# Weight sums of the FFN's fast products: which engine forms them, and in which order

## The chip, the cores and the metric

The kernel runs on 1 core of one Trainium2 chip. The time is device time of one execution in microseconds (us), and the time of a version is the median of its runs. Engines: PE is TensorE, DVE VectorE, ACT ScalarE, POOL GpSimd, SP SyncE, whose queue issues the loads. PEld is PE's weight load.

## The reference

Two layers over a sequence of 256 tokens with 2048 channels, each a mixer and a SwiGLU FFN with norms around them. The change touches the FFN alone:

```python
def swiglu(h, w_gate, w_up, w_down):          # 2048 -> 5632 -> 2048
    return (jax.nn.silu(h @ w_gate) * (h @ w_up)) @ w_down

h = rms_norm(x, norm_ffn_pre[layer])
f = swiglu(h, ffn_w_gate[layer], ffn_w_up[layer], ffn_w_down[layer])
x = x + rms_norm(f.astype(x.dtype), norm_ffn_post[layer])
```

## The kernel before

**Precision.** Every 512x512 weight tile is loaded as f32 (1 MiB, `raw`), copied by ACT to `w_hi` (L1051, `hi`), and DVE takes the rest as `w_lo` (L1791, `lo`). The left operand is split too, and a product is three passes, hi x hi, w_lo x hi, w_hi x lo, of 4 matmuls with 512 columns for each half of the tokens. There are 4 `w_hi` and 3 `w_lo` buffers, so `hi` of a unit waits for the unit four before it and `lo` for the one three before it.

**The FFN.** Its 5632 hidden channels are 11 blocks of 512. The first goes through the ordinary path (the head), the other 10 are bodies. A body computes gate and up of its block (2048 x 512 each) for 2 token tiles by seven-product (Strassen-like) 2x2 forms in place of eight: products P1 to P7, each over two pairs of weight tiles, A (rows 0 and 1) and B (rows 2 and 3). A quarter product (L1635, printed by the tiles sc, pv or acc of L1490) is 12 matmuls. Then the gated tile of the block before is transposed (`turn`, L1701, matmuls of L1504), and multiplied with four tiles of w_down, d0 to d3 (`down`, L1676, L1696), 24 matmuls each. A body has 14 quarter products, 4 downs and 8 transposes. The order of the 18 units is written out in `ENTRIES` (L100) and in the lists of each engine.

**Weight sums.** Of the weight tiles g0 to g3 and u0 to u3 the products need running sums, formed in the raw buffer itself: P5 = g(first) + u(first), P6 adds u(second), P4 adds g(second); P7 = u(first) + u(second). So there are 8 sums a body. `form` (L1794, L1804) does one on DVE; `transfer` (L2333, L2347) does one by an accumulating DMA from SBUF to SBUF that POOL issues. Before: four by `FORMS` (P5A, P6A, P6B, P4B) and four by `TRANSFERS` (P5B, P7A, P7B, P4A).

**Buffers.** 8 raw buffers serve the 12 loads of a body. `place_loads` (L586) gives each load, in the order of `LOADS`, the buffer whose tile is released first by the plan; SP waits for that release and issues in order.

**First bodies.** A layer's first body has lists of its own (`first_block`), since the left operands' combinations S1 to S4 for both pairs are formed there: `left_total`, `left_high` on ACT (L1267) and `left_low` on DVE (L1855, L1857), which all later bodies reuse. ACT's `copy` (L1291) moves a bank's partial result aside, `unload` (L1317) drains a down's bank to `yacc`, `seed` (L1309) writes it back as the start of the next body's down. `head_end` (L343) is the order of the two units ahead of the first body.

Of the kernel before, what the change touches and what calls it, by code (L numbers as in the profile page):

```python
# [51 lines left out]
RAW, HI, LO = 3, 4, 3  # L52
# [34 lines left out]
class Slot:  # L87


    def __init__(self, u, kg, n, first, last, w, cb=0, region="h", layer=0):  # L90
# [69 lines left out]
def loads_of(body):  # L160

    return FIRST_LOADS[len(EARLY):] if body.first else LOADS

# [179 lines left out]
def head_end(slots, body):  # L343
# [16 lines left out]
    tasks += half(gate, 1) + gate.post + half(up, 0) + [Task("early_load", src=body, what=name) for name in EARLY[2:]] + [total(TOTALS[3]), Task("spill", 2 * body.layer + 1, slot=up)]  # L360
    tasks += high_ahead(gate.u, up) + half(up, 1) + low_ahead(gate.u, up) + up.post
# [224 lines left out]
def place_loads(plan):  # L586
# [25 lines left out]
    for part in plan.parts:  # L612
        for task in part.tasks or ():
            if task.kind == "early_load":
                take((task.src.index, task.what), range(RAW) if task.what in EARLY[2:] else (RAW + EARLY.index(task.what),), released(task.src, task.what))
            elif task.kind == "tile_unit" or task.kind == "half" and task.t == 0 and task.passes[0] == 0:
                take(task.slot.u, (POST_GAIN,) if task.slot.u in plan.last_ups else range(RAW), (("lo", task.slot.u + 1, task.slot.u),))
# [12 lines left out]
def trunk(nc, x, norm_mix_pre, norm_mix_post, norm_ffn_pre, norm_ffn_post,  # L630
# [9 lines left out]
    with ExitStack() as ctx:  # L640
# [378 lines left out]
        def _(act):  # L1019
# [299 lines left out]
            def block(body):  # L1319
# [8 lines left out]
                unload(body.prev, 2, 0)  # L1328
                seed(body, 0, 1)
                unload(body.prev, 2, 1)  # L1330
                high(body, "P5A")
                seed(body, 1, 0)
                block_high(body, 0)
                block_high(body, 1)
                high(body, "d1")
                copy(body, "P1")
                high(body, "P5B")
                unload(body, 0, 0)
                seed(body, 1, 1)
                unload(body, 0, 1)  # L1340
                high(body, "P6A")
                seed(body, 3, 0)
                high(body, "P6B")
                unload(body, 1, 0)
                seed(body, 3, 1)
                unload(body, 1, 1)
                high(body, "P3B")
                high(body, "P7A")
                copy(body, "P5")
                seed(body, 2, 0)  # L1350
# [4 lines left out]
                high(body, "d3")  # L1355
# [4 lines left out]
                unload(body, 3, 0)  # L1360
                seed(body, 2, 1)
                unload(body, 3, 1)
                high(body, "d2")
                if body.next:
                    seed(body.next, 0, 0)
                high_next("P1B")
                high_next("P1A")
                silu_part(body, 0)
                silu_part(body, 1)
                high_next("d0")  # L1370

            def first_block(body):

                block_high(body, 0)
                block_high(body, 1)
                high(body, "P5A")
                left_high("S1B", body.layer)
                high(body, "d1")
                unload(body, 0, 0)
                high(body, "P5B")  # L1380
                unload(body, 0, 1)
                copy(body, "P1")
                left_high("S2A", body.layer)
                left_high("S4A", body.layer)
                high(body, "d3")
                high(body, "P6A")
                unload(body, 1, 0)
                high(body, "P6B")
                unload(body, 1, 1)
                copy(body, "P5")  # L1390
                left_high("S2B", body.layer)
                left_high("S4B", body.layer)
                high(body, "P3B")
                high(body, "P7A")
                left_high("S3A", body.layer)
                left_high("S3B", body.layer)
                high(body, "P7B")
                copy(body, "P6")
                high(body, "P3A")
                high(body, "P2A")  # L1400
                high(body, "P4A")
                copy(body, "P7")
                high(body, "P2B")
                unload(body, 3, 0)
                unload(body, 3, 1)
                high(body, "P4B")
                high(body, "d2")
                seed(body.next, 0, 0)
                high(body.next, "P1B")
                high(body.next, "P1A")  # L1410
                silu_part(body, 0)
                silu_part(body, 1)
                high(body.next, "d0")
# [984 lines left out]
```

## Time and profile before

| | us |
|---|---|
| median of 3 runs | 2158.71 (2158.47 to 2160.74) |
| the profiled execution | 2158.62 |
| its span in the profile | 2156.8 |
| PE busy | 2141.2 |
| DVE busy | 1698.2 |
| ACT busy | 1489.6 |
| POOL busy | 230.7 |

The FFN bodies run from 422 to 1030 us and from 1516 to 2124 us. A timeline row gives the start, the duration from the first start to the last end of the merged instructions, engine, line, operation, what is written from what, the count, and in brackets idle time ahead with what ended it. Matmuls overlap, so the distance of two starts says more of PE than a duration.

### The profile page before, as it was taken

How to read it: one execution, taken by the hardware profiler on the slowest of the kernel's cores; microseconds unless marked ns; L12 is line 12 of the kernel's file. 1: busy time of each engine (PE TensorE's matmuls, PEld its weight loads, DVE VectorE, ACT ScalarE, POOL GpSimd, SP SyncE). 2: the span in 40 equal slices, each digit the busy share in tenths (PEclk: the TensorE clock that was granted, in tenths of full speed). 3: DMA queues.
4: the chain of work that ended last, by engine and by line, in shares of the span. 5: the costliest groups of instructions: out<-in, count | busy, mean ns of one | idle time of the engine just before them, and what ended most of it. 6: DMA issues, size and time to landing. Idle time of an engine off the chain costs nothing.

```text
span 2156.8 us, 26554 instructions
## 1 busy us (share of the span) xinstructions
PE 2141.2 (99%) x9771; PEld 1765.4 (82%) x9771; DVE 1698.2 (79%) x1538; ACT 1489.6 (69%) x1774; POOL 230.7 (11%) x274
## 2 busy tenths in 40 slices
PE   9999999999999999999999999999999999999998
PEld 7888888888888888888887787788888888888886
DVE  5577466898898888888755656678998888888886
ACT  6677544787777777777655555447777777777774
POOL 0851000000000000000021001001000000000001
PEclk9999999999999999999999999999999999999999
DMA  9545445799989999997564454557999999998993
GB/s 315 189 154 194 145 148 198 255 290 298 266 256 263 282 296 276 285 289 230 183 215 146 149 169 143 177 175 239 278 299 273 275 292 279 281 292 266 263 263 149
DMA packets 226559, 508.82 MB, mean 236 GB/s; under 512 B 13736, under 2 KB 16384, under 8 KB 214656
## 3 DMA queue, kind: packets, MB, share of 16 engines
q1 hardware_dynamic: 214192, 422.68, 55.6%
q0 software_dynamic: 11520, 83.89, 19.7%
q8 instruction: 79, 1.29, 0.2%
q10 hardware_dynamic: 720, 0.56, 0.1%
q14 instruction: 48, 0.39, 0.0%
HBM read 416.92 MB, written 6.29 MB: 196 GB/s over the span
## 4 chain that ended last, share of the span: by engine, by line
PE 95%; DVE 2%; issue 1%; ACT 1%; DMA 1%; SPq 0%; ACTq 0%; POOLq 0%; POOL 0%; DVEq 0%
PE acc L1477 34%; PE acc L1696 20%; PE sc L1490 20%; PE pv L1490 10%; PE acc L1490 5%; PE tp L1504 3%; PE sc L1590 1%; DVE w_lo L1791 1%; PE pv L1619 1%; PE sc L1586 1%; PE pv L1614 1%; DMA raw<-in_ev_w_in 0%; PE sc L1569 0%; PE pv L1569 0%; ACT h_hi L1097 0%
## 5 line engine op out<-in xcount | busy, mean ns | idle before, releaser
L1791 DVE TENSOR_TENSOR w_lo<-raw,w_hi 128x2048 fp32r<-128x2048 f32 x263 | 601.6, 2293 | 100.2 <-PE acc L1477 41.5
L1051 ACT ACTIVATE w_hi<-raw 128x2048 fp32r<-128x2048 f32 x263 | 503.7, 1916 | 120.4 <-PE acc L1477 45.6
L1477 PE MATMUL acc<-w_hi,h_hi 128*128 128x512 f32 x936 | 261.4, 401 | 2.6 <-ACT h_hi L1021 2.6
L1477 PE MATMUL acc<-w_lo,h_hi 128*128 128x512 f32 x936 | 252.2, 391 | 0.2
L1477 PE MATMUL acc<-w_hi,h_lo 128*128 128x512 f32 x936 | 251.1, 390 | 0.0
L1791 DVE TENSOR_TENSOR w_lo<-xs,w_hi 128x2048 fp32r<-128x2048 f32 x88 | 201.2, 2288 | 31.3 <-PE acc L1696 20.4
L1477 PEld LDWEIGHTS acc<-w_lo,h_hi 128*128 128x128 f32 x936 | 175.6, 188 | 38.9 <-DVE w_lo L1791 1.4
L1477 PEld LDWEIGHTS acc<-w_hi,h_lo 128*128 128x128 f32 x936 | 175.5, 188 | 37.0
L1477 PEld LDWEIGHTS acc<-w_hi,h_hi 128*128 128x128 f32 x936 | 171.1, 189 | 37.0 <-issue 5.5
L1051 ACT ACTIVATE w_hi<-xs 128x2048 fp32r<-128x2048 f32 x88 | 168.5, 1915 | 23.9 <-PE acc L1490 8.1
L1317 ACT ACTIVATE yacc<-acc 128x512 f32<-128x512 f32 x160 | 95.0, 595 | 113.3 <-PE acc L1696 113.3
L1696 PE MATMUL acc<-w_hi,y_lo 128*128 128x512 f32 x640 | 171.0, 389 | 0.0
L1696 PE MATMUL acc<-w_hi,y_hi 128*128 128x512 f32 x640 | 171.0, 389 | 0.0
L1696 PE MATMUL acc<-w_lo,y_hi 128*128 128x512 f32 x640 | 171.0, 389 | 0.0
L1791 DVE TENSOR_TENSOR w_lo<-gq,w_hi 128x2048 fp32r<-128x2048 f32 x54 | 123.5, 2288 | 24.4 <-PE acc L1696 19.6
L1696 PEld LDWEIGHTS acc<-w_hi,y_hi 128*128 128x128 f32 x640 | 120.1, 188 | 24.9
L1696 PEld LDWEIGHTS acc<-w_lo,y_hi 128*128 128x128 f32 x640 | 120.1, 188 | 24.9
L1696 PEld LDWEIGHTS acc<-w_hi,y_lo 128*128 128x128 f32 x640 | 120.1, 188 | 24.9
L1791 DVE TENSOR_TENSOR w_lo<-queries,w_hi 128x2048 fp32r<-128x2048 f32 x50 | 114.4, 2287 | 15.5 <-PE acc L1696 10.2
L1051 ACT ACTIVATE w_hi<-gq 128x2048 fp32r<-128x2048 f32 x54 | 103.5, 1917 | 23.6 <-DVE gq L1804 11.6
L1791 DVE TENSOR_TENSOR w_lo<-gx,w_hi 128x2048 fp32r<-128x2048 f32 x46 | 105.2, 2288 | 15.6 <-PE acc L1696 10.2
L1490 PE MATMUL sc<-w_hi,h_hi 128*128 128x512 f32 x400 | 108.9, 394 | 0.0
(299 smaller groups left out, 3615.6 us busy)
## 6 DMA issues: line engine op xcount, KB each, us to landing
raw<-in_od_w_in SPq DMA_DIRECT2D x48, 1024.0 KB, 5.1
raw<-in_ffn_w_gate SPq DMA_DIRECT2D x38, 1024.0 KB, 9.7
raw<-in_ev_w_in SPq DMA_DIRECT2D x37, 1024.0 KB, 5.3
raw<-in_ffn_w_up SPq DMA_DIRECT2D x36, 1024.0 KB, 7.8
raw<-in_ffn_w_down SPq DMA_DIRECT2D x36, 1024.0 KB, 6.6
xs<-in_ffn_w_up SPq DMA_DIRECT2D x22, 1024.0 KB, 8.0
xs<-in_ffn_w_down SPq DMA_DIRECT2D x18, 1024.0 KB, 7.2
xs<-in_ffn_w_gate SPq DMA_DIRECT2D x18, 1024.0 KB, 10.2
```

Of the source, the lines that this page charges most:

```text
L1051: act.activation(w_hi[u % HI][:, :, :], raw[place.buf][:, :, :], ACT.Copy).then_inc(hi_done, 1)
L1317: act.activation(yacc[:, t, j * KC:(j + 1) * KC], down_banks[k], ACT.Copy).then_inc(drained[k], 1)
L1477: mm = pe.matmul(acc[n % 2][t][:, :], operand(lhs, a, k, t), w[:, k, :], start=first and k == 0 and j == 0, stop=last and k == KT - 1 and ...
L1490: mm = pe.matmul(bank, a[:, k, :], w[:, k, :], start=start and k == 0 and j == 0, stop=stop and k == KT - 1 and j == 2, skip_group_check=c ...
L1504: ins = pe.transpose(dst, src, ident[:, :])
L1586: mm = pe.matmul(sc[:, t, :], q[:, kt, t * P:(t + 1) * P], k[:, kt, task.i % 2, :], start=True, stop=True)
L1590: mm = pe.matmul(sc[:, :, :].rearrange("p m t -> p (m t)"), q[:, kt, t * P:(t + 1) * P], k[:, kt, :, :].rearrange("p m t -> p (m t)"), sta ...
L1614: mm = pe.matmul(pv[:, 0, t * HD:(t + 1) * HD], probT[:, j, t * P:(t + 1) * P], v[:, j, task.i * HD:(task.i + 1) * HD], start=j == 0, stop ...
L1619: mm = pe.matmul(pv[:, 0, 0:CV], flat_pt[:, j * P:(j + 1) * P], v[:, j, hd * CV:(hd + 1) * CV], start=j == 0, stop=j == 1)
L1696: mm = pe.matmul(down_banks[k], a[:, kt, t * P:(t + 1) * P], w[:, kt, :], start=body.first and i == 0 and kt == 0, stop=i == 2 and kt == K ...
L1791: dve.tensor_tensor(w_lo[u % LO][:, :, :], raw[plan.place[u].buf][:, :, :], w_hi[u % HI][:, :, :].bitcast(F32), ALU.subtract).then_inc(lo_ ...
```

## The change

Three sums of a body go by accumulating DMA (P7B, P7A, P4B), five on DVE (P5A, P5B, P6A, P6B, P4A). P5A's sum is formed one body ahead, for a first body in the head. The units get another order: P1A first, the transposes split (four behind P1A, four behind P1B), downs in the order d1, d0, d2, d3, three of them early and d3 at the end. Loads, seeds, unloads, copies and the first half of the gating follow that order. The first body and the others no longer have different load lists.

```diff
-ENTRIES = ("P1B", "P1A", "d0", "P5A", "d1", "P5B", "P6A", "P6B", "P3B",
-           "P7A", "P7B", "P3A", "P2A", "d3", "P4A", "P2B", "P4B", "d2")
-FIRST_ENTRIES = ("P1B", "P1A", "d0", "P5A", "d1", "P5B", "d3", "P6A", "P6B", "P3B",
-                 "P7A", "P7B", "P3A", "P2A", "P4A", "P2B", "P4B", "d2")
-DOWNS = ("d0", "d1", "d3", "d2")
-LOADS = ("d0", "g2", "u2", "g0", "u1", "u0", "d1", "u3", "g1", "g3", "d3", "d2")
-FIRST_LOADS = ("d0", "g2", "u2", "g0", "u0", "d1", "u1", "u3", "d3", "g1", "g3", "d2")
-EARLY = FIRST_LOADS[:4]
-FORMS = ("P5A", "P6A", "P6B", "P4B")
-TRANSFERS = ("P5B", "P7A", "P7B", "P4A")
+ENTRIES = ("P1A", "P1B", "d1", "P5A", "P5B", "d0", "P6A", "d2", "P6B",
+           "P3B", "P3A", "P7A", "P7B", "P2A", "P4A", "P2B", "P4B", "d3")
+FIRST_ENTRIES = ("P1A", "P1B", "d1", "P5A", "d0", "P5B", "d2", "P6A", "P6B",
+                 "P3B", "P3A", "P7A", "P7B", "P2A", "P4A", "P2B", "P4B", "d3")
+DOWNS = ("d1", "d0", "d2", "d3")
+LOADS = ("g2", "g0", "u0", "d1", "u2", "d2", "u3", "d0", "u1", "g3", "g1", "d3")
+EARLY = LOADS[:3]
+FORMS = ("P5A", "P5B", "P6A", "P6B", "P4A")
+FORMS_AHEAD = FORMS[:1]
+TRANSFERS = ("P7B", "P7A", "P4B")
...
-    tasks += high_ahead(gate.u, up) + half(up, 1) + low_ahead(gate.u, up) + up.post
+    tasks += high_ahead(gate.u, up) + half(up, 1)
+    tasks += [Task("form", src=body, what=name) for name in FORMS_AHEAD] + up.post + low_ahead(gate.u, up)
```

The new lists that the prediction walks through: DVE's of a middle body, and the ends of the first body's on DVE and ACT.

```python
# DVE, block
gated(body.prev, 1)
low(body, "d1")
form(body, "P5B")
block_low(body, 0)
low(body, "P5A")
block_low(body, 1)
low(body, "P5B")
form(body, "P6A")
low(body, "d0")
form(body, "P6B")
low(body, "P6A")
low(body, "d2")
low(body, "P6B")
low(body, "P3B")
form(body, "P4A")
low(body, "P3A")
low(body, "P7A")
low(body, "P7B")
low(body, "P2A")
upper_part(body, 0)
low(body, "P4A")
low(body, "P2B")
upper_part(body, 1)
low(body, "P4B")
low(body, "d3")
low_next("P1A")
if body.next:
    form(body.next, "P5A")
gated(body, 0)
low_next("P1B")
```

```python
# DVE, first_block, from P3B on      # ACT, first_block, from P3B on
low(body, "P3B")                     # high(body, "P3B")
low(body, "P3A")                     # high(body, "P3A")
left_low("S3A", body.layer)          # copy(body, "P6")
low(body, "P7A")                     # left_high("S3A", body.layer)
left_low("S3B", body.layer)          # left_high("S3B", body.layer)
low(body, "P7B")                     # high(body, "P7A")
form(body, "P4A")                    # high(body, "P7B")
low(body, "P2A")                     # high(body, "P2A")
```

## Rows read from the trace of the kernel before

**Rows 1.** The page: header, busy time of engines, chain by engine.
```profile
span 2156.8 us, 26554 instructions
...
PE 2141.2 (99%) x9771; PEld 1765.4 (82%) x9771; DVE 1698.2 (79%) x1538; ACT 1489.6 (69%) x1774; POOL 230.7 (11%) x274
...
PE 95%; DVE 2%; issue 1%; ACT 1%; DMA 1%; SPq 0%; ACTq 0%; POOLq 0%; POOL 0%; DVEq 0%
```

**Rows 2.** Timeline of PE, a middle body's turn, and the next one's.
```profile
911.48 1.03 PE L1504 MATMUL tp<-ident,tok 128*128 128x128 f32 x8
912.27 1.17 PE L1490 MATMUL sc<-w_hi,h_hi 128*128 128x512 f32 x4
913.27 1.07 PE L1490 MATMUL sc<-w_lo,h_hi 128*128 128x512 f32 x4
914.18 1.07 PE L1490 MATMUL sc<-w_hi,h_lo 128*128 128x512 f32 x4
...
972.21 1.03 PE L1504 MATMUL tp<-ident,tok 128*128 128x128 f32 x8
```

**Rows 3.** Windows: stretch, then busy us of each engine, clock, DMA share, GB/s.
```profile
422.50:486.40 63.90, 63.80 (x286) 52.53 (x285) 62.04 (x42) 46.33 (x43) 3.46 (x4) 1.00 0.93 290
911.70:972.40 60.70, 60.70 (x274) 50.34 (x273) 53.16 (x28) 47.01 (x43) 3.48 (x4) 1.00 0.92 277
```

The engines of a windows row are PE, PEld, DVE, ACT and POOL in this order; the first row is a first body, the second a middle one.

**Rows 4.** Timeline of PE, product P4A of the first body, layer 0.
```profile
469.60 1.07 PE L1490 MATMUL sc<-w_hi,h_hi 128*128 128x512 f32 x4
470.77 1.20 PE L1490 MATMUL sc<-w_lo,h_hi 128*128 128x512 f32 x4
...
473.65 1.07 PE L1490 MATMUL acc<-w_lo,h_hi 128*128 128x512 f32 x4
```

**Rows 5.** Timeline of DVE in that first body.
```profile
423.33 2.28 DVE L1791 TENSOR_TENSOR w_lo<-gx,w_hi 128x2048 fp32r<-128x2048 f32 x1
...
431.33 2.29 DVE L1791 TENSOR_TENSOR w_lo<-raw,w_hi 128x2048 fp32r<-128x2048 f32 x1 [0.78 <-ACT w_hi L1051]
...
443.07 2.29 DVE L1804 TENSOR_TENSOR queries<-queries,xs 128x2048 f32<-128x2048 f32 x1
...
456.22 0.69 DVE L1857 TENSOR_TENSOR lefts<-prob,lefts 128x512 fp32r<-128x512 f32 x1
456.82 2.28 DVE L1791 TENSOR_TENSOR w_lo<-raw,w_hi 128x2048 fp32r<-128x2048 f32 x1
...
464.03 2.28 DVE L1791 TENSOR_TENSOR w_lo<-gq,w_hi 128x2048 fp32r<-128x2048 f32 x1
466.23 2.28 DVE L1804 TENSOR_TENSOR queries<-queries,gx 128x2048 f32<-128x2048 f32 x1
468.44 2.28 DVE L1791 TENSOR_TENSOR w_lo<-raw,w_hi 128x2048 fp32r<-128x2048 f32 x1
```

**Rows 6.** Timeline of PE, transposes in runs of four at the layer boundary.
```profile
1078.57 0.38 PE L1504 MATMUL tp<-ident,xs 128*128 128x128 f32 x2
...
1078.92 1.18 PE L1477 MATMUL acc<-w_hi,h_hi 128*128 128x512 f32 x4
1079.94 1.08 PE L1477 MATMUL acc<-w_lo,h_hi 128*128 128x512 f32 x4
```

**Rows 7.** The page: DMA queues, packets, MB, share of 16 engines' span.
```profile
q1 hardware_dynamic: 214192, 422.68, 55.6%
q0 software_dynamic: 11520, 83.89, 19.7%
```

**Rows 8.** Timeline of ACT in the first body.
```profile
457.73 0.57 ACT L1291 ACTIVATE probT<-sc 128x512 f32<-128x512 f32 x1
458.20 1.91 ACT L1051 ACTIVATE w_hi<-xs 128x2048 fp32r<-128x2048 f32 x1
```

**Rows 9.** Line L904, all weight loads: from issue to landing.
```profile
DMA to landing us min/median/max: 4.9/7.2/17.3
```

**Rows 10.** Timeline of PE, behind the last transposes of layer 0's FFN.
```profile
1031.65 1.17 PE L1477 MATMUL acc<-w_hi,y_hi 128*128 128x512 f32 x4 [0.39 <-ACT y_hi L1260]
```

More of the change, by code:

```diff
@@ L160, in loads_of @@
 def loads_of(body):
-    return FIRST_LOADS[len(EARLY):] if body.first else LOADS
+    return tuple(name for name in LOADS if not (body.first and name in EARLY))
 class Part:
@@ L1326, in high_next @@
                         hi(u)
-                unload(body.prev, 2, 0)
-                seed(body, 0, 1)
[L1330 to L1337, printed above, removed]
+                unload(body.prev, 3, 0)
+                seed(body, 1, 1)
+                unload(body.prev, 3, 1)
@@ new lines, in block @@
+                high(body, "P5A")
+                seed(body, 0, 0)
+                block_high(body, 0)
+                high(body, "P5B")
+                block_high(body, 1)
+                high(body, "d0")
+                unload(body, 1, 0)
+                copy(body, "P1")
+                seed(body, 0, 1)
+                unload(body, 1, 1)
+                seed(body, 2, 0)
+                high(body, "P6A")
+                high(body, "d2")
+                copy(body, "P5")
+                high(body, "P6B")
@@ L1348, in block @@
                 high(body, "P7A")
-                copy(body, "P5")
-                seed(body, 2, 0)
                 high(body, "P7B")
                 copy(body, "P6")
-                high(body, "P3A")
+                high(body, "P2A")
+                high(body, "P4A")
+                if body.next:
+                    seed(body.next, 1, 0)
+                high(body, "P2B")
+                copy(body, "P7")
+                high(body, "P4B")
+                high(body, "d3")
+                high_next("P1A")
@@ L1359, in block @@
                 high(body, "P4B")
[L1360 to L1367, printed above, removed]
+                unload(body, 2, 0)
+                unload(body, 2, 1)
+                high(body, "d3")
+                seed(body.next, 1, 0)
+                high(body.next, "P1A")
+                high(body.next, "P1B")
                 silu_part(body, 0)
                 silu_part(body, 1)
[L1370 to L1413, printed above, removed]
+                high(body.next, "d1")
             act.dma_start(pre[:, :, :], pre_T).then_inc(pre_in, 16)
@@ L1426, in _ @@
                     block(body)
-                unload(part.bodies[-1], 2, 0)
-                unload(part.bodies[-1], 2, 1)
+                unload(part.bodies[-1], 3, 0)
+                unload(part.bodies[-1], 3, 1)
                 for t in range(NT):
@@ L1751, in first_block @@
                     quarter_product(body, "P4B")
-                    down(body, 2)
+                    down(body, 3)
+                def first_block(body):
+                    quarter_product(body, "P1A")
+                    turn(body, 0)
+                    quarter_product(body, "P1B")
+                    turn(body, 1)
+                    down(body, 1)
+                    quarter_product(body, "P5A")
+                    down(body, 0)
+                    quarter_product(body, "P5B")
+                    down(body, 2)
+                    quarter_product(body, "P6A")
+                    quarter_product(body, "P6B")
+                    quarter_product(body, "P3B")
+                    quarter_product(body, "P3A")
+                    quarter_product(body, "P7A")
+                    quarter_product(body, "P7B")
+                    quarter_product(body, "P2A")
+                    quarter_product(body, "P4A")
+                    quarter_product(body, "P2B")
+                    quarter_product(body, "P4B")
+                    down(body, 3)
                 first_block(part.bodies[0])
@@ L2199, in first_block @@
                 low(body, "P3B")
+                low(body, "P3A")
                 left_low("S3A", body.layer)
@@ L2352, in _ @@
                 for body in section.bodies or ():
-                    transfer(body, "P5B")
+                    transfer(body, "P7B")
                     transfer(body, "P7A")
-                    transfer(body, "P7B")
-                    transfer(body, "P4A")
+                    transfer(body, "P4B")
 def log_counts():
```

134 lines of the change are left out of this document (69 added, 65 removed).

## The prediction

> **What bounds the kernel now.** I read the page's header first: TensorE (PE) is busy 2141.2 us of the 2156.8 us span, and the chain that ended last is 95% PE [rows 1]; the granted clock of the bodies is 1.00, the 2.4 GHz level [rows 3]. Busy time can hide waiting inside long matmuls, so the next view is PE's timeline of one late FFN body: groups of four 512-column matmuls start every 0.907 us (226.7 ns each) with no idle in brackets, across products and downs alike [rows 2]. One body is 66 such groups and 8 transposes, 66 x 0.907 + 0.88 = 60.7 us, and the two turns of neighbouring bodies lie exactly that far apart (911.48 and 972.21) [rows 2]. So 18 of the 20 bodies hold no PE stall that a better feed could take away. The windows view of such a body says who is nearest to becoming the bound: VectorE (DVE) 53.16 us of 60.70, the DMA engines 92%, ScalarE (ACT) 47.01 [rows 3]. The first body of a layer is tighter: DVE 62.04 of 63.90 [rows 3]. There PE does stall once: the w_hi group starts at 469.60, the w_lo group at 470.77 instead of 470.51, and the fourth group behind 469.60 is at 473.65 instead of 473.23: 0.42 us late in all, restart included [rows 4]. The w_lo it waits for ended at 470.72, right behind a weight sum (466.23) in front of it [rows 5]. This is seen once per layer. So in the part that the diff touches, before can give back 2 x 0.42 = 0.8 us, and no more.
>
> **The change, part by part.** (1) *Matmuls.* The number is unchanged: 14 quarter products of 12 and 4 downs of 24 in each body. Only the order differs. No gain, no loss.
>
> (2) *The turn of the gated tile.* Before, its 8 transposes are one run; after, 4 stand behind P1A and 4 behind P1B. The run of 8 takes from 911.48 to 912.27, and the group after the next starts 1.00 us on instead of 0.907: 0.79 + 0.10 = 0.89 us [rows 2]. Runs of four stand at the layer boundary: 1078.57 to 1078.92, then 1.02 us, so 0.35 + 0.11 = 0.46, and 0.47 with the last hundredth of the restart [rows 6]. Two of them cost 0.94, so a body is 0.047 us longer, 20 bodies 0.9 us. This is on PE and nothing hides it. Bounds: 0 if the two runs cost what one does, 2 us if a restart costs 0.1 us.
>
> (3) *Weight sums.* One accumulating DMA per body goes, one VectorE sum comes. The DMAs of the Pool queue took 19.7% of 16 engines' span for 80 transfers [rows 7]: 0.197 x 2156.8 / 80 = 5.3 us of all engines each, a load of 1 MiB on SP's queue, of which 422.68 MB are 403, 0.556 x 2156.8 / 403 = 3.0 [rows 7]. A body falls from 12 x 3.0 + 4 x 5.3 = 57 us to 52 of 60.8. Nothing on PE waits for this, so it is worth nothing by itself. A sum is 2.28 us, and starts of such instructions follow each other by 2.20 [rows 5]. DVE becomes 53.2 + 2.3 = 55.5 us of 60.8 in a middle body. Total time fits; what counts is each deadline. A w_lo is wanted 0.91 us after its unit's first matmul, and may start only when the unit three before it is finished.
>
> (4) *Middle bodies (18).* I laid the new PE order out from 0: P1A 0, P1B 3.19, d1 6.38, P5A 11.82, P5B 14.54, d0 17.26, P6A 22.70, d2 25.42, P6B 30.86, P3B 33.58, then one product every 2.72 us up to P4B 52.62, and d3 55.34; next body 60.78. Under it I put DVE's list at 2.20 us for each long and 0.60 for each short instruction [rows 5], and ACT's at 0.1 us less than the duration, 1.82 for a w_hi and 0.47 for a copy [rows 8]. Every w_lo ends at least 3.4 us ahead of its deadline: the least is d0 (ends 14.8, wanted 18.2), then P4A and P4B 3.7. The five sums lie where the three long downs d1, d0, d2 give DVE 8.2 us beyond the products' pace: P5A at 55.1 of the body before, P5B 2.5, P6A 10.3, P6B 14.7, P4A 27.9. ACT's least margin is copy P7 (45.3 for P4A at 47.2) and the second y_hi (7.2 for 9.1). Stall: 0. Each w_hi has its form or transfer in time too: transfer P7B can go at 5, P7A at about 10, P4B at 25, and their totals are wanted from 31.6, 33.9 and 45.2 on. They no longer overlap the eight loads that go between 36 and 53.
>
> The one load with a short lead is u1: its buffer is d1's, free at 2.6, and its sum P6A is due at 10.3. The quickest weight load lands 4.9 us after its issue [rows 9], and by 3.0 us each the backlog of eight loads is drained at about 2. It can slip 3.4 us before d0's w_lo is late.
>
> (5) *First bodies (2).* DVE has 14 sums and low parts of the combined left operands besides. Before, it runs from 431.33 with no idle in brackets [rows 5]. After, form P5A is done in the head, in the place of one w_lo, and P1B's w_lo takes the place at 423.33 [rows 5]. From there to form P6B stand 8 long and 4 short instructions: 8 x 2.20 + 4 x 0.60 = 20.0, so P6B's sum starts at 443.33, before at 443.07: 0.26 late. The same instructions as before follow up to P3B. Then ACT: its new list has copy P6 ahead of P7A's w_hi, and it waits for product P6B. Five products lie between P6B and P4A, whose first matmul is at 469.60 [rows 4]: 469.60 + 0.05 (one more split turn) - 5 x 2.72 = 456.05, and 0.16 until the last matmul is out (1.07 long, 0.907 apart) [rows 2] with 0.05 for the signal: 456.25. Copy 0.47, two left parts at 0.53 (my value, a little above the copy), w_hi 1.91: it ends at 459.69. DVE is free at 456.22 + 0.26 + 2.20 + 0.60 = 459.28 [rows 5], so another 0.44 is lost, signal included. Then P4A's sum, which before stood behind P2A (466.23), stands in front of it: 2.20. P2A's w_lo ended at 466.31 before; after, 466.31 + 0.26 + 0.44 + 2.20 = 469.21. PE wants it at 469.60 + 0.05 - 2.72 + 0.91 = 467.84 [rows 4]. Stall 1.37 + 0.05 for the signal + 0.16 restart [rows 4] = 1.58 us. The stall itself covers P4A's w_lo (ends 472.0, wanted 472.1), and DVE stays 2 us late into the next body, inside its 3.4. The old stall of 0.42 goes. Net 1.16 us a layer, 2.3 us in all. Bounds: -0.8 (no stall at all) and +5 (another copy or sum comes late too).
>
> (6) *Head and tail.* u0 is loaded in place of u2 and the spill is issued one load earlier; form P5A reads u0 some 18 us after that issue, more than the slowest load needs [rows 9]: 0. In the tail PE waits 0.39 us for y_hi behind the eight transposes [rows 10], behind an unload of the last down on ACT, and that sequence stays: 0. The second tail slot's load moves to the buffer of g2, free at 49.8; it lands at 55, which delays the two SiLUs to 58.2 and the second gated half to 61.1, just before its transposes at 61.2. Cost 0, up to 0.5 us a layer if I am wrong by that much.
>
> **Sum.** 0.9 + 2.3 = 3.3 us on PE's path (rounded). The profiled execution took 2158.62 us (span 2156.8 and 1.8 around it), 0.1 below the median of 2158.71. 2158.7 + 3.3 = 2162.0 us.
>
> **A rule against the row.** PE's matmul rows fill 99% and its weight loads 82% [rows 1]. The Trainium skill (Trainium Kernel Development and Optimization, Performance Expectations) says that matmul busy time is a bad metric because matmuls are pipelined, and that the busy share of LDWEIGHTS is the good one. By it 18% of the span would be slack. The trace disagrees for the bodies: the groups keep a beat of 0.907 us whichever engine is early or late, with 512 columns for each weight load, so the 18% is the weight path waiting for the array. If the rule held here, the DMA time taken away could come back as time; that is the rival below with 3%.
>
> **Rivals.** *A, first bodies cost less:* DVE gains the 0.3 to 0.4 us that I add, or a later start of a neighbouring product hides it. Then only the turns and a short stall remain: 2159 to 2161 us. For it: my margins there are tenths. Chance 25%.
> *B, slower by a feed that comes late in the middle bodies:* u1 lands later than 13.7 us into the body, form P6A holds DVE, and d0's and P6A's w_lo slip. Place: DVE's form P6A. Decides from 3.4 us of lateness; each 0.3 us beyond it costs 0.3 x 18 = 5.4 us, so 2165 to 2180. For it: beside transfers, a load can need far longer than alone (the slowest weight load 17.3 us against 4.9 at best) [rows 9]; against: only P7B's transfer can be in flight then, and starts 3 us after u1. Chance 15%.
> *C, faster:* both stalls of the first bodies go and the tail or the matmuls gain, by the rule above or by less DMA traffic beside PE. More than 4.3 us isn't in the trace, where all PE idle in the touched part is about 2 us. 2154 us; 3%.
> *D, the change does not do what it says:* the sum costs nothing visible since it runs under PE, and the time is that of the turns alone, 2159.6. Within A's range; counted there.
>
> **How the numbers follow.** The forecast, 2161 to 2164, has 57%, A 25%, B 15%, C 3%. What a measurement of this kernel can tell from no change is about 0.2%, 4.3 us, so the line lies at 2163.0. The forecast puts a third of its weight above the line (0.57 x 0.3 = 0.17), B all of its 0.15: slower 0.32. C gives faster 0.03. Same is the rest, 0.65. The range 2159 to 2167 takes in A, the forecast and the near end of B, and leaves out C and the long end of B.
>
> **What would show it.** PE timeline: groups of 0.907 us in middle bodies, turns 60.78 apart, no idle in brackets. DVE timeline: 23 long instructions per body, idle about 6 us. First body: P2A's w_lo group starts about 1.4 us late behind form P4A; nothing at P4A. A stall at d0 or P6A in middle bodies, or DVE waiting for a DMA of u1, means B. Stall-free first bodies mean A.

## The result, and the profile after

The changed kernel takes 2164.3 us (median of 15 runs, 2163.5 to 2164.9) and the kernel before 2159.76 us beside it (15 runs): a ratio of 1.0022, 95% interval 1.0015 to 1.0029, some 4.5 us more. The forecast was 2162.0 with a range of 2159 to 2167. The time lies inside the range, but 0.3 us above the band of 2161 to 2164 to which the prediction gave 57%. The whole interval lies above 1, so the change does cost time. The middle of the interval is 0.02% past the 0.2% line that the prediction drew between "same" (0.65) and "slower" (0.32), and the interval has both sides of it, so the measurement does not decide between these two. The profiled executions give the difference in one number: a span of 2161.7 us against 2156.8 [rows 1], 4.9 us.

From the page of the changed kernel (header, busy times, the Pool queue's DMAs):

```profile
span 2161.7 us, 26536 instructions
...
PE 2142.6 (99%) x9771; PEld 1762.8 (82%) x9771; DVE 1741.5 (81%) x1558; ACT 1491.5 (69%) x1774; POOL 218.8 (10%) x254
...
q0 software_dynamic: 8640, 62.92, 14.7%
```

The number of PE's matmuls is the same, 9771. DVE has 20 instructions and 43 us more, the Pool queue 20 transfers less (62.92 MB after 83.89 [rows 7]). Each transfer still takes 0.147 x 2161.7 / 60 = 5.3 us of all DMA engines. The windows (columns as in rows 3) show the same stretches:

```profile
422.50:486.40 63.90, 62.61 (x280) 51.37 (x279) 63.49 (x42) 47.35 (x44) 2.78 (x3) 1.00 0.84 260
911.70:972.40 60.70, 60.70 (x273) 50.26 (x272) 55.16 (x30) 47.08 (x43) 2.60 (x3) 1.00 0.84 260
```

A middle body has DVE at 55.16 us (forecast 55.5) and the DMA share at 0.84 after 0.92 [rows 3]; PE is busy without a gap. In the first body PE is idle for 1.29 of the 63.90 us (0.10 before), and DVE is busy for 63.49 of them.

**Where the 4.9 us are.** In both kernels a body is 272 PE instructions, in another order. So I took the start of the n-th instruction from each trace at the borders of the bodies and looked at how the difference between the traces grows from border to border. This sees hundredths of a microsecond, where a ratio has an interval of 1 to 2 us to either side. Ahead of the first body the runs differ by -0.3 to +1.9 us, all but 0.1 of it in the first 116 us (the start of the loads), which the edits don't touch; I leave it out below. Two words return: the beat is the 0.907 us from one group of four matmuls to the next, and a restart is what the groups behind a pause or behind transposes take beyond the beat. Growth of the difference to the kernel before, in us (layer 0 / layer 1), for all kernels of this study:

| kernel | first body | second body | each further body | end of layer |
|---|---|---|---|---|
| changed kernel | +1.31 / +1.33 | +0.29 / +0.29 | +0.07 | +0.77 / +0.02 |
| copy behind P7A | +0.83 / +0.85 | +0.32 / +0.27 | +0.07 | +0.79 / -0.04 |
| P4A by DMA, issued last | +2.29 / +3.67 | +0.37 / +0.07 | +0.07 | +0.76 / -0.04 |
| P4A by DMA, ahead of P4B | -0.35 / -0.35 | +0.07 / +0.07 | +0.07 | +0.93 / -0.02 |
| the same in all bodies | -0.35 / -0.35 | +0.07 / +0.07 | +0.07 | +1.07 / -0.04 |
| turns together | +1.24 / +1.27 | +0.29 / +0.25 | 0.00 | +0.70 / 0.00 |
| s3's load first | +1.29 / +1.31 | +0.32 / +0.29 | +0.07 | -0.03 / -0.04 |
| second y_hi first | +1.34 / +1.33 | +0.07 / +0.07 | +0.07 | +0.82 / -0.02 |
| d0's w_lo twice | +1.29 / +1.33 | +1.08 / +1.03 | +0.07 | +0.69 / +0.01 |
| d0's w_lo thrice | +1.33 / +1.29 | +3.39 / +5.05 | +1.50 / +1.55 | +0.73 / -0.02 |
| all four edits | -0.42 / -0.42 | 0.00 / 0.00 | 0.00 | 0.00 / 0.00 |

Line numbers of the changed kernel are one higher than before (w_lo is L1792, w_hi L1052, the sum L1805). Its first body, PE's timeline (start, duration, engine, line, what is written from what, count, idle ahead), then DVE's and ACT's:

```profile
466.73 1.07 PE L1491 MATMUL acc<-w_hi,h_hi 128*128 128x512 f32 x4
469.09 1.19 PE L1491 MATMUL acc<-w_lo,h_hi 128*128 128x512 f32 x4 [1.29 <-DVE w_lo L1792]
```

```profile
459.53 2.29 DVE L1792 TENSOR_TENSOR w_lo<-raw,w_hi 128x2048 fp32r<-128x2048 f32 x1 [0.37 <-ACT w_hi L1052]
...
464.54 2.29 DVE L1805 TENSOR_TENSOR queries<-queries,gq 128x2048 f32<-128x2048 f32 x1
466.75 2.29 DVE L1792 TENSOR_TENSOR w_lo<-gq,w_hi 128x2048 fp32r<-128x2048 f32 x1
```

```profile
456.05 0.60 ACT L1292 ACTIVATE probT<-sc 128x512 f32<-128x512 f32 x1 [1.02 <-PE sc L1491]
```

This is the stall that was forecast, at P2A's w_lo, behind the sum P4A (464.54), which stands behind a w_lo that lost 0.37 us to ACT, whose copy (456.05) was early in its list. What I had at nothing was the second body (ACT's timeline, then PE's):

```profile
491.41 1.92 ACT L1052 ACTIVATE w_hi<-raw 128x2048 fp32r<-128x2048 f32 x1 [2.74 <-DVE raw L1805]
493.24 0.58 ACT L1261 ACTIVATE y_hi<-tp 128x512 fp32r<-128x512 f32 x1
```

```profile
492.93 1.07 PE L1697 MATMUL acc<-w_hi,y_lo 128*128 128x512 f32 x4
493.96 1.16 PE L1697 MATMUL acc<-w_hi,y_hi 128*128 128x512 f32 x4
```

The groups of d1 start 1.03 us apart where 0.91 is the beat: PE wants y_hi at 493.84 (492.93 + 0.91), and it ended at 493.82, to which the signal is added. It stands in ACT's list behind a w_hi that waited 2.74 us for DVE's sum P5B. And the end of layer 0 (PE, then ACT, then DVE, then the issues of SP's queue):

```profile
1043.71 1.07 PE L1478 MATMUL acc<-w_hi,y_lo 128*128 128x512 f32 x4
1045.26 1.17 PE L1478 MATMUL acc<-w_hi,y_hi 128*128 128x512 f32 x4 [0.48 <-issue]
```

```profile
1039.72 1.92 ACT L1052 ACTIVATE w_hi<-raw 128x2048 fp32r<-128x2048 f32 x1 [5.75 <-DMA raw<-in_ffn_w_down]
```

```profile
1041.66 2.29 DVE L1792 TENSOR_TENSOR w_lo<-raw,w_hi 128x2048 fp32r<-128x2048 f32 x1 [1.50 <-ACT w_hi L1052]
1043.87 1.28 DVE L1912 TENSOR_TENSOR yacc<-acc,yacc 128x512 f32<-128x512 f32 x2
```

```profile
1021.26 3.00 SPq L905 DMA_DIRECT2D raw<-in_ffn_w_down  x2
...
1024.86 1.18 SPq L899 DMA_DIRECT2D xs<-out  x2
1026.61 0.38 SPq L905 DMA_DIRECT2D raw<-in_ffn_w_down  x1
```

The last w_down tile (slot s3) is issued at 1026.61 behind two other tiles and the two reloads of xs. ACT gets it at 1039.72, 13.1 us later. DVE's w_lo then holds up the adds from 1043.87 on, which read the `acc` bank and end at 1045.15; PE's next group starts at 1045.26, 1.55 us after the one before it and not 0.91. The profile names no engine for this wait; that it is for the adds is my reading of these times. In the kernel before, SP's queue had the reloads out earlier and only this tile behind them:

```profile
1019.72 2.91 SPq L898 DMA_DIRECT2D xs<-out  x2
1024.65 0.38 SPq L904 DMA_DIRECT2D raw<-in_ffn_w_down  x1
```

### The profile page after: what moved, and what is told of

It reads as the page before. It is cut to its first block, busy times and chain, and to the rows that moved or that the text cites. A ratio compares the mean times of both kernels' runs of the same rounds, so it can differ in the third digit from the quotient of the medians.

```text
span 2161.7 us, 26536 instructions
## 1 busy us (share of the span) xinstructions
PE 2142.6 (99%) x9771; PEld 1762.8 (82%) x9771; DVE 1741.5 (81%) x1558; ACT 1491.5 (69%) x1774; POOL 218.8 (10%) x254
## 3 DMA queue, kind: packets, MB, share of 16 engines
q0 software_dynamic: 8640, 62.92, 14.7%
q8 instruction: 79, 1.29, 0.2%
## 4 chain that ended last, share of the span: by engine, by line
PE 95%; DVE 1%; ACT 1%; DMA 1%; issue 1%; SPq 1%; ACTq 0%; POOLq 0%; POOL 0%; DVEq 0%
PE acc L1478 33%; PE acc L1697 20%; PE sc L1491 20%; PE pv L1491 10%; PE acc L1491 5%; PE tp L1505 3%; PE sc L1591 1%; PE pv L1620 1%; PE sc L1587 1%; DVE w_lo L1792 1%; PE pv L1615 1%; DMA raw<-in_ev_w_in 1%; PE sc L1570 0%; PE pv L1570 0%; ACT h_hi L1098 0%
## 5 line engine op out<-in xcount | busy, mean ns | idle before, releaser
L1792 DVE TENSOR_TENSOR w_lo<-raw,w_hi 128x2048 fp32r<-128x2048 f32 x281 | 644.3, 2295 | 106.7 <-PE acc L1478 41.0
L1052 ACT ACTIVATE w_hi<-raw 128x2048 fp32r<-128x2048 f32 x281 | 537.6, 1915 | 122.6 <-PE acc L1478 38.2
L1792 DVE TENSOR_TENSOR w_lo<-xs,w_hi 128x2048 fp32r<-128x2048 f32 x84 | 191.8, 2289 | 20.4 <-PE sc L1491 6.7
L1052 ACT ACTIVATE w_hi<-xs 128x2048 fp32r<-128x2048 f32 x84 | 160.2, 1914 | 19.1 <-PE sc L1491 8.3
L1792 DVE TENSOR_TENSOR w_lo<-gq,w_hi 128x2048 fp32r<-128x2048 f32 x48 | 109.9, 2289 | 12.1 <-PE acc L1697 4.9
L1491 PE MATMUL sc<-w_hi,h_lo 128*128 128x512 f32 x400 | 107.3, 390 | 0.0
L1491 PE MATMUL sc<-w_lo,h_hi 128*128 128x512 f32 x400 | 107.2, 390 | 0.0
L1792 DVE TENSOR_TENSOR w_lo<-gx,w_hi 128x2048 fp32r<-128x2048 f32 x44 | 100.6, 2287 | 7.7 <-PE sc L1491 2.6
```

The costliest lines, as they stand in the source:

```text
L1052: act.activation(w_hi[u % HI][:, :, :], raw[place.buf][:, :, :], ACT.Copy).then_inc(hi_done, 1)
L1491: mm = pe.matmul(bank, a[:, k, :], w[:, k, :], start=start and k == 0 and j == 0, stop=stop and k == KT - 1 and j == 2, skip_group_check=c ...
L1792: dve.tensor_tensor(w_lo[u % LO][:, :, :], raw[plan.place[u].buf][:, :, :], w_hi[u % HI][:, :, :].bitcast(F32), ALU.subtract).then_inc(lo_ ...
```

## The experiments

**Theory:** the 4.9 us are the sum of four causes that don't depend on each other: (a) the turns in two runs, 20 x 0.073 = 1.5 us; (b) the first bodies' stall by DVE's chain (copy, sum P4A), 2 x 1.24 = 2.5; (c) the second bodies' 2 x 0.22 = 0.4 by ACT's wait for the sum P5B; (d) slot s3's late load, 0.8. **Rivals:** the feed as a whole got tighter (DVE's busy share), so that removing one wait uncovers another; or the change of DMA traffic has a price or a worth of its own. All edits are made on the changed kernel. The times are medians with ratios to the kernel before, which ran beside each.

### The copy of P6 behind P7A's w_hi

```diff
-                copy(body, "P6")
                 left_high("S3A", body.layer)
                 left_high("S3B", body.layer)
                 high(body, "P7A")
+                copy(body, "P6")
                 high(body, "P7B")
```

> The changed kernel with one step of ScalarE moved: in the first body of each layer the copy of P6 stands behind P7A's w_hi instead of ahead of it. Theory (the stall ahead of P2A is the sum of three delays on VectorE's chain: 0.4 us of copy, 2.2 us of form P4A, 0.3 us of shift): the stall of 1.29 us ahead of P2A's w_lo group falls to 0.9 us in each of the two first bodies, and the 0.2 us that follow in the second body shrink with it; the whole is 0.7 to 1.1 us shorter than the changed kernel, 2163.2 to 2163.6 us beside a kernel before of 2159.8. Rival (form P4A alone sets the stall, because VectorE would be as late with or without the copy): stall unchanged at 1.3 us, time 2164.3 us.

Measured: 2163.52 us, ratio 1.0021 (1.0012 to 1.0030). PE's timeline:

```profile
467.14 1.07 PE L1491 MATMUL acc<-w_hi,h_hi 128*128 128x512 f32 x4
469.04 1.20 PE L1491 MATMUL acc<-w_lo,h_hi 128*128 128x512 f32 x4 [0.83 <-DVE w_lo L1792]
```

The ratio can't be told from the changed kernel's 1.0022; the traces show the difference. The stall fell from 1.29 to 0.83 us, and the first bodies by 0.48 each: the copy's share of the chain, as forecast. The second bodies did not shrink with it (0.32 and 0.27). I should have seen that: once PE has waited for DVE's w_lo, PE's own clock is set by DVE, so DVE is just as late against PE behind a short stall as behind a long one.

### P4A's sum of the first bodies by a DMA again

The core of the edit (the sum leaves DVE's list in `first_block`, the counts of the semaphores follow it):

```diff
-                form(body, "P4A")
...
                     transfer(body, "P4B")
+                    if body.first:
+                        transfer(body, "P4A")
```

> The changed kernel, but in the first body of each layer P4A's sum is formed by an accumulating DMA as in the kernel before, and not on VectorE; the other bodies keep it on VectorE. Theory: the stall ahead of P2A (1.3 us), the one in the second body (0.2 us behind form P5B and ScalarE's wait on it), both with their restarts, are all from this form. Both go, and some 3.0 to 3.5 us of the 4.5 come back: about 2161.0 us beside a kernel before of 2159.8. The second body then has no gap over 0.05 us ahead of block_high's second half. Rival (the stall at P2A is only moved, because the transfer of P4A lands too late under the new order and holds a w_hi of ScalarE up, or VectorE's queue is late anyway): a gap of 0.5 us or more stays in front of P2A or P4A, and the time stays within 1 us of 2164.3.

Measured: 2166.77 us in 5 runs, ratio 1.0034 (1.0021 to 1.0046). The interval overlaps that of the changed kernel (1.0015 to 1.0029), but in the traces the bodies take 3.2 us more than there. The rival held. POOL's timeline, ACT's and PE's:

```profile
454.35 0.85 POOL L2354 DMA_DIRECT2D gx<-xs  x1 [19.62 <-DVE w_lo L1796]
454.90 1.21 POOL L2354 DMA_DIRECT2D queries<-gq  x1
```

```profile
469.05 1.91 ACT L1056 ACTIVATE w_hi<-queries 128x2048 fp32r<-128x2048 f32 x1 [5.45 <-DMA queries<-gq]
```

```profile
471.50 1.20 PE L1495 MATMUL sc<-w_hi,h_hi 128*128 128x512 f32 x4 [1.39 <-ACT rgx L1296]
473.35 1.20 PE L1495 MATMUL sc<-w_lo,h_hi 128*128 128x512 f32 x4 [0.65 <-DVE w_lo L1796]
```

P2A's stall is gone, but the transfer of P4A is issued behind P4B's, which had waited for DVE until 454.35, and lands 14.1 us later, at 469.03, 5.45 us after ACT wants it. Two stalls at P4A stand for the one at P2A. In layer 1 the first body loses 3.67 us and not 2.29, though PE stands no longer there (1.24 and 0.65 us idle, 1.39 and 0.65 in layer 0). What differs is TensorE's clock behind the second stall, in this windows row (columns as in rows 3):

```profile
1571.20:1574.00 2.80, 2.80 (x8) 2.19 (x7) 2.80 (x3) 2.80 (x4) 0.00 (x0) 0.50 1.05 387
```

The granted clock is 0.50 there, the 1.2 GHz level, and a matmul takes 427 ns; from 474 to 478 us, behind the same stall in layer 0, it is 1.00. The two groups behind the stall take 1.5 us more for it. Why it fell in one layer alone is open. So putting P4A on DVE was not a loss of 2.5 us against a free alternative: under the new order a transfer at this place of POOL's list costs more.

### The same transfer ahead of P4B's

```diff
+                    if body.first:
+                        transfer(body, "P4A")
                     transfer(body, "P4B")
-                    if body.first:
-                        transfer(body, "P4A")
```

> As the run in which the first bodies form P4A by an accumulating DMA, with one difference: that transfer is issued ahead of P4B's instead of behind it. There it was issued at 454.90 us, 0.55 us behind P4B's, and landed after 14.1 us at 469.03; ScalarE's w_hi of P4A had waited 5.45 us for it and TensorE stood at 469.7 to 471.5 and 472.3 to 473.35. Theory (the transfer was late because it was queued last, behind P4B's, whose product comes last of all): P4A's lands by 464, P4B's, now last, by 470, which is before ScalarE wants it; no gap is left in the first body, and with the 0.22 us of the second body gone as well the time is 3.0 to 3.7 us under the changed kernel's 2164.3: 2160.6 to 2161.3 us. Rival (two transfers so close behind each other share the DMA engines with the loads, and whichever is second or both land late): a gap of 1 us or more stays at P4A's or P4B's w_hi, and the time stays over 2163 us.

Measured: 2160.96 us, ratio 1.0008 (0.9999 to 1.0017). POOL's timeline, and the w_hi of P4A and of P4B on ACT:

```profile
452.19 0.85 POOL L2354 DMA_DIRECT2D queries<-gq  x1 [17.18 <-DMA gq<-in_ffn_w_gate]
454.81 0.88 POOL L2354 DMA_DIRECT2D gx<-xs  x1 [1.78 <-DVE w_lo L1796]
```

```profile
463.90 1.91 ACT L1056 ACTIVATE w_hi<-queries 128x2048 fp32r<-128x2048 f32 x1
...
470.13 1.91 ACT L1056 ACTIVATE w_hi<-gx 128x2048 fp32r<-128x2048 f32 x1
```

P4A's inputs are ready before P4B's, so its transfer also starts earlier (452.19 us), and the next one is issued 2.6 us and not 0.55 us behind it: order and distance change together. Neither w_hi waits for a transfer now, and PE keeps its 0.907 us beat through both products. The first bodies are 0.35 us shorter than before the change (the old stall of 0.42 [rows 4] is gone, less 0.07 for the turns), and the second ones cost only the turns. Against the changed kernel that is 1.88 and 1.90 us a layer, 3.8 in all; the ratios give 0.14%, 3.0 us. The sum on DVE was the whole of (b) and (c).

### P4A's sum by DMA in all bodies

The same two edits without `if body.first`: four sums by DMA and four on DVE, under the new order.

> P4A's sum by an accumulating DMA ahead of P4B's in all 20 bodies: the split four and four of the kernel before, under the order of the changed kernel. Theory (the fifth sum on VectorE is worth nothing and costs nothing in the 18 middle bodies; it only costs in the first ones): the same time as with P4A by DMA in the first bodies alone, 2160.6 to 2161.3 us, with the 0.073 us a body of the turns still in it. Rival (the DMA engines' 5 us a body less do matter, because loads land earlier): slower than that by 0.1 us a body or more, 2 us in all.

Measured: 2161.14 us, ratio 1.0010 (1.0001 to 1.0019), beside 1.0008 for the run above. The window of the middle body:

```profile
911.70:972.40 60.70, 60.70 (x273) 50.26 (x272) 52.96 (x29) 47.06 (x43) 3.51 (x4) 1.00 0.94 277
```

A middle body has DVE at 52.96 us in place of 55.16 and the DMA share at 0.94 in place of 0.84, and its length is the same to 0.01 us. Neither the 2.2 us of DVE nor the tenth of the DMA engines is worth anything there. The end of layer 0 costs 0.1 to 0.4 us more than in the other runs that keep s3's load behind the reloads, which I did not follow up.

### Both turns together

```diff
                     turn(body, 0)
+                    turn(body, 1)
                     quarter_product(body, "P1B")
-                    turn(body, 1)
```

> The changed kernel, but TensorE does both turns (8 transposes) in one run behind each other again instead of 4, then P1B, then 4. Theory A (the prediction's): only the transposes themselves cost more in two runs, 0.047 us a body: 20 bodies give 0.9 us back, 2163.4 us. Theory B (from the trace of the changed kernel: the matmul groups behind each restart run at 0.92 instead of 0.907 us for a few groups more, 0.073 us a body): 1.5 us come back, 2162.8 us. Rival (putting the turns together makes the second half of P1 or ScalarE's y_hi late): 1 us or more is lost.

Measured: 2162.96 us, ratio 1.0017 (1.0008 to 1.0026). PE's timeline of a middle body, first of the changed kernel, then of this one:

```profile
913.29 0.60 PE L1505 MATMUL tp<-ident,tok 128*128 128x128 f32 x4
913.65 1.18 PE L1491 MATMUL sc<-w_hi,h_hi 128*128 128x512 f32 x4
914.67 1.08 PE L1491 MATMUL sc<-w_lo,h_hi 128*128 128x512 f32 x4
915.59 1.09 PE L1491 MATMUL sc<-w_hi,h_lo 128*128 128x512 f32 x4
916.51 0.60 PE L1505 MATMUL tp<-ident,tok 128*128 128x128 f32 x4
916.87 1.18 PE L1697 MATMUL acc<-w_hi,y_hi 128*128 128x512 f32 x4
```

```profile
913.14 1.03 PE L1505 MATMUL tp<-ident,tok 128*128 128x128 f32 x8
913.93 1.17 PE L1491 MATMUL sc<-w_hi,h_hi 128*128 128x512 f32 x4
914.94 1.07 PE L1491 MATMUL sc<-w_lo,h_hi 128*128 128x512 f32 x4
915.84 1.07 PE L1491 MATMUL sc<-w_hi,h_lo 128*128 128x512 f32 x4
```

A middle body is as long as before the change, to 0.01 us: theory B. By the table 1.3 us come back and not 20 x 0.073 = 1.5, because the second bodies give back only 0.00 and 0.04: there PE waits for y_hi in either order. Of the 0.073, 0.04 is the second run (0.79 becomes 2 x 0.36, and one restart of 0.11 more), for which the forecast had 0.047. The rest is two groups behind the first run that take 0.92 us each (914.67, 915.59, 916.51) where the long run is followed by 0.90 and 0.91.

### Slot s3's load ahead of the reloads

```diff
-    tasks[i + 1:i + 1] = [Task("gains", b), Task("reload", b)]
+    tasks[i + 1:i + 1] = [Task("gains", b)]
+    j = next(i for i, task in enumerate(tasks) if task.kind == "half" and task.slot is nxt and task.t == 0)
+    tasks.insert(j + 1, Task("reload", b))
```

> The changed kernel, but at the end of layer 0 the queue issues the load of slot s3 (w_down) ahead of the two reloads of xs instead of behind them. Theory (the 0.77 us lost at the boundary of the layers come from that load, which landed at 1039.7 instead of 1032.0 and held ScalarE's w_hi up by 5.75 us): it lands by 1035, the wait is under 1 us, and the gap at 1044.7 goes: 0.6 to 0.8 us shorter, 2163.6 us beside a kernel before of 2159.8. Rival (the gap comes from VectorE's queue, which carries one sum more than before, and not from the load): gap and time unchanged, or the reloads, now later, open one of their own behind the boundary.

Measured: 2163.22 us, ratio 1.0020 (1.0011 to 1.0029). ACT's timeline and PE's:

```profile
1035.08 1.92 ACT L1054 ACTIVATE w_hi<-raw 128x2048 fp32r<-128x2048 f32 x1 [0.42 <-DMA raw<-in_ffn_w_down]
```

```profile
1045.28 1.07 PE L1480 MATMUL acc<-w_hi,y_hi 128*128 128x512 f32 x4
```

The w_hi starts at 1035.08 in place of 1039.72, PE's gap is gone, and the end of layer 0 costs -0.03 us in place of +0.77. The reloads, now behind it, open no gap. The load itself is issued no earlier: 1027.31 us in a trace that runs 0.7 us later at this place, for 1026.61. So cause (d) is the order in SP's queue, the 2 MiB of reloads ahead of this load, and not the moment of its issue.

### The second y_hi ahead of P5B's w_hi, in the second bodies

```diff
-                high(body, "P5B")
-                block_high(body, 1)
+                if body.prev.first:
+                    block_high(body, 1)
+                    high(body, "P5B")
+                else:
+                    high(body, "P5B")
+                    block_high(body, 1)
```

> The changed kernel, but in the second body of each layer ScalarE does its second y_hi ahead of P5B's w_hi, which waits 2.74 us for VectorE's form P5B (491.41 us). The transposes that y_hi reads end at 491.14 us. Theory (the 0.29 us that the second body costs, 0.07 of it from the turns, come from y_hi standing behind that wait): it ends by 491.9 instead of 493.82, the start of the second half at 493.96 moves up by 0.2, and the second body costs 0.07 us: 0.44 us less in all. Rival (the 0.22 us come from VectorE's own late w_lo and y_lo): the second body still costs 0.29 us.

Measured: 2163.9 us in one run. A single run can't show 0.44 us in the time, so the trace has to. It runs 0.8 us later at this place than the changed kernel's. ACT's timeline and PE's:

```profile
492.04 0.60 ACT L1261 ACTIVATE y_hi<-tp 128x512 fp32r<-128x512 f32 x1 [2.59 <-PE tp L1509]
```

```profile
493.70 1.08 PE L1701 MATMUL acc<-w_hi,y_lo 128*128 128x512 f32 x4
494.61 1.07 PE L1701 MATMUL acc<-w_hi,y_hi 128*128 128x512 f32 x4
```

The second bodies cost 0.07 us each in place of 0.29, with DVE as late as ever: cause (c) was ACT's order, y_hi standing behind the wait for DVE's sum.

### Margins: d0's w_lo written twice and three times

In `block` (18 bodies) DVE repeats the subtraction of d0's w_lo into the same buffer, so nothing is left out (2 is the number of repeats, 1 in the milder run):

```diff
-                low(body, "d0")
+                lo(body.u["d0"], 2)
```

Three times:

> The changed kernel with work added, and the same output: in the 18 middle bodies VectorE writes d0's w_lo three times instead of once (+4.5 us a body, so that it is busy 59.6 of 60.7 us). Theory (what decides is the margin at each product, 3.4 us at d0 with 925.34 to 928.76 us, and not the busy share): d0's w_lo comes 1.1 us late, TensorE stands once in each body, 1.1 to 1.2 us with the restart, 20 to 22 us in all: about 2185 us. Rival A (the 5.5 us of idle time in each body absorb it): 2164 us. Rival B (the delay also carries on to ScalarE through form P6B and to the next body): 4 us and more a body, over 2230 us.

Measured: 2196.4 us in one run, 11 us more than the theory had. DVE's timeline and PE's in a body:

```profile
936.64 4.61 DVE L1794 TENSOR_TENSOR w_lo<-gq,w_hi 128x2048 fp32r<-128x2048 f32 x2
941.28 2.29 DVE L1798 TENSOR_TENSOR w_lo<-gq,w_hi 128x2048 fp32r<-128x2048 f32 x1
```

```profile
941.44 1.07 PE L1698 MATMUL acc<-w_hi,y_hi 128*128 128x512 f32 x4
943.62 1.19 PE L1698 MATMUL acc<-w_lo,y_hi 128*128 128x512 f32 x4 [1.12 <-DVE w_lo L1798]
```

The mechanism is the expected one, one stall a body, at d0 and nowhere else, but it costs 1.43 us and not 1.1 to 1.2. The added work is 941.28 - 936.64 = 4.64 us (a repeat waits for the write before it), and without it the w_lo would have ended at 941.28 + 2.29 - 4.64 = 938.93. PE wants it at 941.44 + 0.91 = 942.35: a margin of 3.42, and 1.22 us late by what is added. With the signal PE starts at 943.62, 1.27 late. Behind it come 0.16 of restart. The second bodies lose much more (3.39 and 5.05 us). In layer 0 the 2 us by which DVE enters the body late explain it about (4.64 + 2 - 3.42 = 3.2). In layer 1 PE stands at d0 no longer (2.78 us idle, 2.82 in layer 0), but the matmuls behind the stall are slower:

```profile
1620.50:1623.00 2.50, 2.50 (x7) 1.93 (x6) 2.50 (x2) 2.01 (x2) 0.00 (x0) 0.50 0.94 354
```

This windows row has the granted clock at 0.50, as in the first body of the run with P4A's transfer issued last; in layer 0 it is 1.00 from 508 to 512 us, behind the same stall. The three groups behind the stall take 1.6 us more at this clock, which is the difference between the layers.

Twice:

> As the run in which the 18 middle bodies write d0's w_lo three times, but twice (+2.3 us a body instead of +4.5; same output). There a body cost 1.5 us, all of it at d0. Theory (3.4 us of margin at d0): d0's w_lo still comes 1.1 us ahead of its matmuls, form P6B ends at 929.8 instead of 927.5 and ScalarE's w_hi of P6B starts 1.3 us late, with 5 us of margin to its product: nothing in a middle body, 2164.3 us. Only the second body of each layer, into which VectorE comes 2 us late, has 4.3 us of 3.4 used up and stands for 0.9 to 1.2 us at d0: up to 2.4 us in all. Rival (any added VectorE time costs a share of itself): 0.75 us a body, 13 us.

Measured: 2166.34 us in one run. In the middle bodies the added 2.3 us cost 0.00, in the second bodies 0.79 and 0.74 more than in the changed kernel. PE's timeline there:

```profile
503.58 1.07 PE L1698 MATMUL acc<-w_hi,y_hi 128*128 128x512 f32 x4
505.12 1.20 PE L1698 MATMUL acc<-w_lo,y_hi 128*128 128x512 f32 x4 [0.47 <-DVE w_lo L1798]
```

So the margin at d0 lies between 2.3 and 4.6 us of DVE time, as the 3.4 says, and the price is nothing up to it, and past it the lateness itself and a restart of 0.16 us. The rival "a share of each added microsecond" is out.

### All four edits together

P4A of the first bodies by a DMA ahead of P4B's, the copy behind P7A's w_hi, the turns together, slot s3's load first.

> All four edits on the changed kernel: P4A of the first bodies by a DMA that is issued ahead of P4B's, the copy of P6 behind P7A's w_hi, both turns together again, slot s3's load ahead of the reloads. If the four causes are apart and add up: 2164.3 - 3.3 (first and second bodies) - 1.46 (turns, 0.073 times 20) - 0.76 (slot s3) = 2158.8 us, 1.0 us under the kernel before (ratio 0.9995), since the 0.42 us that the kernel before loses in each first body goes too. Rival (they hide each other: a stall that is taken away uncovers the next one): 2160 us or more, with a gap that the kernel before does not have.

Measured: 2158.45 us, ratio 0.9998 (0.9989 to 1.0007): no difference from the kernel before that can be measured. In the trace every body but the first ones has the length it had before, to 0.01 us, and the first ones are 0.42 us shorter, which is the kernel before's own stall [rows 4]. The four causes add up, and none hid another: against the changed kernel the table gives 3.48 us of the first bodies, 0.58 of the second, 16 x 0.073 = 1.17 of the further ones and 0.79 of the layers' ends, 6.0 in all, and the ratios 0.24%, 5.2 us. The edits don't add up in the same way: moving the copy gave 0.48 us a first body by itself and gives nothing here, since with the sum gone from DVE the first bodies are free of stalls already (-0.35 without the edit of the copy, -0.42 with it, and 0.07 of that is the turns). Copy and sum are one cause, (b). The 0.84 us that the table has it shorter than the kernel before are below what the comparison of medians resolves.

## Why the prediction was right, and where it was not

- **Bound and matmuls (1):** right. Middle bodies keep the beat; PE has no idle in them.
- **Turns (2):** right in kind, small by a third: 0.073 us a body for 0.047, 1.5 us for 0.9. The term was priced from runs of four at the layer boundary, of which only the first group behind the run was read [rows 6]; the two groups that follow at 0.92 us were not in it, though they stand in the same trace (1079.94 to 1080.86, and on to 1081.79). It was inside the bounds of 0 to 2 us.
- **Sums (3):** right that the moved sum is worth nothing by itself. DMA engines fell from 0.92 to 0.84 of a body, DVE rose to 55.16 us, and the run with P4A by DMA everywhere shows that neither matters.
- **Middle bodies (4):** right, and the margin of 3.4 us at d0 was measured from both sides by the repeats.
- **First bodies (5):** right to hundredths. The copy was put at 456.25 and starts at 456.05 (this trace runs 0.22 us early); P2A's w_lo was to end at 469.21 and ends at 466.75 + 2.29 = 469.04; PE was to stand 1.58 us with its restart and stands 1.66. Net 1.24 a layer for 1.16, turns apart. The 0.44 us for copy P6 ahead of P7A's w_hi measured 0.48.
- **"DVE stays 2 us late into the next body, inside its 3.4":** this step failed, by too little to show in the total. It compared the lateness with DVE's own least margin only. But DVE's form P5B also feeds ACT, and in ACT's list the y_hi of the second half stands behind that w_hi, with a margin of 1.9 us that the prediction's own paragraph on middle bodies names (7.2 for 9.1). 2 us of lateness used it up, and it cost 0.22 us a layer, 0.4 in all.
- **Head and tail (6):** the head cost nothing. The tail was put at 0, up to 0.5 us a layer, for the second tail slot. The 0.77 came in layer 0 alone and from slot s3, whose load I had not followed past the reloads in SP's queue; layer 1, where the same bodies end the run, shows +0.02.
- **Sum:** 3.3 us by the terms; by the table 1.5 + 2.5 + 0.4 + 0.8 = 5.2, less 0.2 of the early part and 0.1 at the very end 4.9. All four terms missed to the same side: turns by 0.6, first bodies by 0.2, second bodies by 0.4, the end of layer 0 by 0.8. The time still lies in the range because the range was wide enough, and not because misses cancelled. Of the 2.3 us between the forecast and 2164.3, 1.1 are the kernel before itself, whose median beside the changed kernel was 2159.76 and not 2158.71.
- **Rivals:** A (first bodies cost less) and D did not happen; B (u1 late in middle bodies) did not happen: in the middle body from 911 to 972 us DVE waits for PE alone, 5.4 us in all, and for no load or transfer. C did not happen either: with the DMA share down from 0.92 to 0.84, a middle body got no shorter, and the weight loads' share stayed at 82%. The Trainium skill (Trainium Kernel Development and Optimization, Performance Expectations) names that share, beside MFU, as a good metric for how close a kernel is to its roofline. Read as slack, which is how the prediction read it, the missing 18% are not borne out by the trace: no feed that was eased brought a middle body below its 66 groups and its transposes.

## What to carry to other kernels

Lateness has to be followed through every engine that waits for the late one, and compared with the least margin of the whole chain, not of the late engine alone. Work given to an engine with idle time cost nothing here up to the margin of the nearest product, and past it the lateness and a restart, so a schedule is read by its margins and not by busy shares. Where an operation moves between a DMA queue and an engine, its place in the new list matters as much as its kind: the same transfer cost a first body 2.6 us more behind its neighbour than ahead of it, and 4.0 where TensorE's clock fell behind the stall. So a stall can cost more than its length, and the granted clock behind it has to be read too. Small costs of several independent causes are best told apart by aligning two traces instruction by instruction.

## What the runs showed of the hardware

- An accumulating 1 MiB transfer in SBUF takes 5.3 us of all DMA engines but its time to landing varied: in the first body of layer 0, beside loads, P4B's took 7.2 us from its issue with no other transfer near it. With two transfers 0.55 us apart they took 7.1 and 14.1 us, and with 2.6 us between the two issues 7.0 and 10.7 us.
- A 1 MiB load issued at the layer's end behind two reloads reached ACT 13.1 us after its issue; issued ahead of them, at 1027.31, by 1035.08, 7.8 us.
- Between two runs of four transposes 3.2 us apart, the second and third groups of matmuls take 0.92 us (230 ns a matmul) and not 0.907. Behind the second of these runs (917.88 to 918.79 in the changed kernel) and behind a run of eight they don't. Why is open.
- Behind a stall of PE the granted clock can fall to 0.50 (1.2 GHz), with 427 ns a matmul for 227: it did in layer 1 behind 2.78 us of idle time (1620.5 to 1623.0 us, d0's w_lo thrice), and behind 1.24 and 0.65 us (1571.2 to 1574.0 us, P4A's transfer issued last). Behind stalls as long in layer 0 of the same runs it stayed at 1.00. It added 1.6 and 1.5 us.
